# A transformer kernel without the products at its norms that nobody reads

## The chip, the cores and the metric

The kernel runs on one core of one Trainium2 chip. The metric is the device time of one launch in microseconds (us). All data are float32.
## What is computed

Two blocks in a row work on one sequence of 512 tokens with 1024 features. The first has two layers (a mixer of RG-LRU and mLSTM, then windowed attention), each with a convolved feed-forward part and a per-layer input; the second has two layers (MLA, then RWKV-7), each between two SwiGLU feed-forward parts, with gains and shifts that come from a conditioning vector. Ahead of every part stands an RMS norm:

```python
def rms_norm(x, g):
    xf = x.astype(jnp.float32)
    y = xf * lax.rsqrt(jnp.mean(xf * xf, axis=-1, keepdims=True) + EPS)
    return (y * g.astype(jnp.float32)).astype(x.dtype)
```

There are thirteen of them in the kernel, numbered 0 to 12. What follows each norm:

| norm | follows | first products on its result |
|---|---|---|
| 0 | mixer's inputs (`hy_in`) | 512 columns |
| 1, 4 | feed-forward, convolved (`up1`, `up4`) | 256 columns, with sums by VectorE |
| 2, 5 | per-layer input (`ple2`, `ple5`) | 512 columns |
| 3 | attention's inputs (`at_in`) | 512 columns |
| 6, 8, 9, 11 | SwiGLU (`up6`, ...) | 256 columns, with sums by VectorE |
| 7 | MLA's inputs (`mla_in`) | 512 columns |
| 10 | RWKV's inputs (`rw_in`) | 512 columns |
| 12 | the output | none |

## The kernel before

Activations lie transposed: features on the 128 partitions in 8 blocks (`X`, the residual, and `H`, the normed), tokens along the 512 columns. Weights stream as tiles of 16 blocks of 128 x 128 through a ring of three buffers (`weight_ring`), issued by SyncE. Each engine runs one program in written order and waits on semaphores; there is no scheduler. TensorE writes to eight PSUM banks.

A norm runs over all engines. ScalarE squares the eight blocks of the residual (`SQ`), VectorE adds the first six squares in `RB` (named `rstd` in rows, as the names go by buffer). TensorE's part is `norm_sum(n)`, from line 925:

- *the sums*: three times four products, over `RB` and the last two squares, each with `pick`, a matrix of 4 columns. In the rows they are 24 records of 4 columns (`constant_matrices,rstd` x8 and `constant_matrices,squares` x16), since a float32 product shows as two records;
- ScalarE takes the square root, VectorE the reciprocal (L2171) into four columns of `small_columns`;
- *the spread*: four products by the identity put it on all partitions (`constant_matrices,small_columns`, 8 records of 128 columns);
- VectorE then scales the eight blocks one after another (L2174), in norms 6 to 11 with a shift, which for block 0 VectorE adds (L2182) and for the others ScalarE. Each block's semaphore lets TensorE start on it.

Between these steps stand products of the identity with a constant matrix, written by the helper `fill(out, *widths)` (line 913): one product for each width (`T` is 512 columns, `HALF` 256), into `bank[0]` or the norm's own bank, before those banks are written anew. They bear no semaphore and wait for none. In norms 2 and 5 `ple_ahead` puts real products (the per-layer input) ahead of the sums and between sums and spread.

After norms 1, 4, 6, 8, 9 and 11 comes `up(n)`. It multiplies 2 x 2 blocks with seven products (`P1` to `P7`) in place of eight: P1 and P2 need normed blocks alone (8 products of 256 columns, 16 records), P6 and P5 need sums of blocks that VectorE makes once all eight blocks are normed (`token_sum`, L2203 to L2209).

Of the kernel before, what the change touches and what calls it, by code (L numbers as in the profile page):

```python
# [14 lines left out]
T = 512  # L15
# [280 lines left out]
CAT, NC = {}, 0  # L296
# [46 lines left out]
def build(nc, io):  # L343
    with ExitStack() as ctx:
        def sb(name, *shape):
            return ctx.enter_context(nc.sbuf_tensor(name, [P, *shape], F32))
# [3 lines left out]
        def S(name):  # L350
            if name not in names:
                names[name] = ctx.enter_context(nc.semaphore(name))
            return names[name]
# [13 lines left out]
        C = sb("constant_matrices", NC)  # L367
# [7 lines left out]
        bank = [ctx.enter_context(nc.psum_tensor(f"bank{b}", [P, T], F32)) for b in range(8)]  # L375
# [4 lines left out]
        def const(name, j=0, n=P):  # L380
            return C[:, CAT[name] + j * n:CAT[name] + (j + 1) * n]
# [9 lines left out]
        def sbank(s):  # L391
            return bank[4 + s % 4]
# [27 lines left out]
        norm_bank = bank[7]  # L420
# [25 lines left out]
        HALF = T // 2  # L446
# [214 lines left out]
        def _(sp):  # L661
# [49 lines left out]
            for n, (_, _) in enumerate(STREAM):  # L711
                if n == 2:
                    sp.dma_start(C[:, EARLY:], io["constants"][:, EARLY:]).then_inc(S("constants_landed"), 16)
                if n == rw_tile + 11:
                    store_low(0)
                    store_low(1)
                if n == rw_tile + 12:
                    store_low(2)
                    store_low(3)
                if n == rw_tile + 15:  # L720
                    store_inverses(0)
                    load_step(0)
                    load_step(1)
                if n == rw_tile + 17:
                    store_inverses(1)
                    for i in range(2, 16):
                        load_step(i)
                if n >= RING:
                    before = STREAM[n - RING][0]
                    if before is None:  # L730
                        sp.wait_ge(tile_used, plain_tiles(n - RING))
                    else:
                        part_is_full(sp, *before, "P4")
                for at, k, tile, place, *quarter in pieces(n):
                    lower = n == rw_tile + 6 and at == 8
                    rows, of = (slice(64, P), slice(0, 64)) if lower else (slice(0, P), slice(0, P))
                    for r in quarter:
                        rows, of = slice(32 * r, 32 * r + 32), slice(0, 32)
                    sp.dma_start(ring[rows, n % RING, at * P:(at + k) * P], tiles[tile][of, place * P:(place + k) * P])\
                        .then_inc(landed[n % RING], 16)  # L740
# [132 lines left out]
        def _(pe):  # L873
            at = {"m": 0, "s": 0, "w": 0, "free_inc": 0, "open": 0}

            def mm(out, lhsT, rhs, start, stop, inc=None):
                i = pe.matmul(out, lhsT, rhs, start=start, stop=stop)  # L877
                if inc is not None:
                    i.then_inc(inc, 1)
                elif at["free_inc"]:  # L880

                    i.then_inc(tile_used, at["free_inc"])
                    at["free_inc"] = 0
# [26 lines left out]
            def begin(name):  # L910
                assert (at["m"], at["s"], at["w"]) == AT[name], (name, at, AT[name])

            def fill(out, *widths):

                for n in widths:
                    pe.matmul(out[:, 0:n], const("ident"), C[:, CAT["sel"]:CAT["sel"] + n], start=True, stop=True)  # L916

            def ple_ahead(n, j):
                pe.wait_ge(S(f"p{n // 3}_landed"), 16)
                part_is_taken(pe, f"down{n - 1}", DB // 2 - 1, ("P7", "P4", "P3")[j])  # L920
                at["w"] = AT[f"ple{n}"][2] + 10 * j + 8
                for k in range(2):
                    mm(bank[4 + j][:, :], weight(), PT[:, k, :], k == 0, k == 1, S("ple_projected") if k else None)

            def norm_sum(n):

                begin(f"norm{n}")
                if at["s"] >= 4:
                    pe.wait_ge(small_done[3], at["s"] // 4)
                if n in (2, 5):  # L930
                    ple_ahead(n, 0)
                    ple_ahead(n, 1)
                if n in (3, 6):
                    fill(norm_bank, T, T)
                for k, x in ((5, RB[:, :]), (6, SQ[:, 0, :]), (7, SQ[:, 1, :])):
                    if k == 5:
                        pe.wait_ge(S("squares_added"), 5 * (n + 1))
                    else:
                        if k == 6 and n == 9:
                            fill(bank[0], T, T)  # L940
                        pe.wait_ge(S("square_ready"), DB * n + k + 1)
                    for t in range(NB):
                        mm(norm_bank[:, 0:NB], x[:, t * P:(t + 1) * P], const("pick", t, NB), k == 5 and t == 0,
                           k == 7 and t == NB - 1, S("norm_summed") if k == 7 and t == NB - 1 else None)
                if n in (2, 5):
                    ple_ahead(n, 2)
                    at["w"] = AT[f"ple{n}"][2]
                elif 0 < n < 12:
                    fill(bank[0], HALF)
                pe.wait_ge(S("rstd_ready"), n + 1)  # L950
                for t in range(NB):
                    mm(norm_bank[:, t * P:(t + 1) * P], RSTD[:, t:t + 1].to_broadcast([P, P]), const("ident"), True, True,
                       S("rstd_spread") if t == NB - 1 else None)
                if 0 < n < 12:
                    fill(bank[0], *((T,) if n < 6 else (T, T, T) if n == 10 else (T, HALF)))

            def project(rhs, kb, ready, cols=P, rows=P):

# [142 lines left out]
            def ple(n):  # L1101
                norm_sum(n)
                begin(f"ple{n}")
                w0 = at["w"]
                for j in range(DB):
                    at["w"] = w0 + 10 * j
                    project(lambda k: H[:, k, :], DB, normed(n) if j == 0 else settled)
                    if j >= AHEAD:
                        project(lambda k: PT[:, k, :], 2, settled)
                at["w"] = w0 + 10 * DB  # L1110
# [3 lines left out]
            for _ in range(5):  # L1114
                pe.matmul(bank[0][:, :], X[:, 0, 0:P], X[:, 0, :], start=True, stop=True)
            pe.wait_ge(S("first_constants_landed"), 16)
            norm_sum(0)
            begin("hy_in")
            h = lambda k: H[:, k, :]
# [92 lines left out]
            for j in range(DB):  # L1212
                project(y, DB, (lambda k: pe.wait_ge(S("y_rg"), k + 1) if k < 4 else pe.wait_ge(S("y_ml"), k - 3))
                        if j == 0 else settled)
            norm_sum(1)
            up(1)
            down(1)
# [40 lines left out]
            for w in range(16 + LAG + 1):  # L1258
                if w < 16:
                    n, g = w // 4, w % 4  # L1260
# [17 lines left out]
                if w >= LAG + 1:  # L1278
                    q = w - LAG - 1
                    n, g = q // 4, q % 4  # L1280
# [3 lines left out]
                    for b in range(0 if n else 1, 2):  # L1284
                        t = n - 1 + b
                        values = A[:, 12 + t // 2, t % 2 * 256 + 64 * g:t % 2 * 256 + 64 * g + 64]
                        for half in range(2):
                            turned = B[:, 12 + (2 * q + half) % 4, :].rearrange("p (e b t) -> p b e t", b=2, t=P)
                            out = sbank(ss[half])[64 * half:64 * half + 64, 0:256].rearrange("p (e t) -> p e t", t=P)
# [55 lines left out]
            for w in range(8 * NB + MLAG + 1):  # L1345
                if w < 8 * NB:
                    n = w % NB
# [15 lines left out]
                if w >= MLAG + 1:  # L1363
                    q = w - MLAG - 1
                    n = q % NB
# [1738 lines left out]
```

## Time and profile before

| | us |
|---|---|
| median of three runs | 4146.09 |
| lowest, highest | 4143.68, 4148.68 |
| the profiled execution | 4144.75 |
| its span, first to last instruction | 4142.9 |
| TensorE busy | 4024.5 (97%) |
| VectorE busy | 1971.4 (48%) |
| GpSimd busy | 1334.7 (32%) |
| ScalarE busy | 669.4 (16%) |
| mean granted clock of TensorE | 0.988 of 2.4 GHz |

Busy time of TensorE holds a modelled tail of each record, so that the records of a dense stretch overlap a little; the distance from start to start is what a record costs there. The windows of rows 2 begin with each norm's sums, at norms 0, 1, 2, 3, 7, 8 and 10; PE, PEld, DVE, ACT and POOL follow in this order. The profile's views used below are the page's parts, one source line's instructions, the timeline of an engine over a window, and sums over windows with the granted clock.

### The profile page before, as it was taken

To read this page: it belongs to the slowest core of one execution; us is meant where nothing else is said; L and a number is where in the kernel's file an instruction comes from. 1 tells how busy PE (TensorE), PEld (TensorE's weight loads), DVE (VectorE), ACT (ScalarE), POOL (GpSimd) and SP (SyncE) were. 2 spreads that over 40 slices of the span, in tenths; PEclk is the share of its full clock that TensorE was granted. 3 is DMA by queue.
4 is the path that set the end of the run, shared out by engine and by line. 5 is a ranking of instruction groups with operands and counts; after the bars stand their busy time and mean duration, and the time that the engine had idled before them with its cause. 6 is when DMAs were issued, how large, how long until landed. Compare 5 with 4: busy or idle time off the path is not lost. (4 is left out here: it accounts for less than half of the span.)

```text
span 4142.9 us, 45459 instructions
## 1 busy us (share of the span) xinstructions
PE 4024.5 (97%) x17988; PEld 3008.5 (73%) x17988; DVE 1971.4 (48%) x3520; ACT 669.4 (16%) x1404; POOL 1334.7 (32%) x1138
## 2 busy tenths in 40 slices
PE   9999999998899999999999999999999989989999
PEld 4448888644488885888844588888888437848888
DVE  5437766448377752433245344324432654434432
ACT  2321110114211101100024310001000321211000
POOL 0004444103244341344303434444443052023443
PEclk9999999999999999999999999999999999999999
DMA  3115454210244442222210122222222232112222
GB/s 130 41 66 188 159 181 163 81 66 24 92 172 173 141 174 72 81 83 89 84 66 21 41 88 85 87 87 82 82 87 87 71 111 63 32 47 92 82 87 76
DMA packets 133058, 386.80 MB, mean 93 GB/s; under 512 B 38800, under 2 KB 45072, under 8 KB 123120
## 3 DMA queue, kind: packets, MB, share of 16 engines
q1 hardware_dynamic: 118064, 305.23, 22.6%
q10 hardware_dynamic: 13968, 75.70, 4.9%
q8 instruction: 144, 2.36, 0.2%
q0 software_dynamic: 816, 2.97, 0.2%
q14 instruction: 66, 0.54, 0.0%
HBM read 375.26 MB, written 8.39 MB: 93 GB/s over the span
## 5 line engine op out<-in xcount | busy, mean ns | idle before, releaser
L877 PE MATMUL bank<-normed,weight_ring 128*128 128x256 f32 (+2 forms) x3376 | 1011.8, 453 | 17.8 <-ACT normed L1690 10.3
L877 PEld LDWEIGHTS bank<-normed,weight_ring 128*128 128x128 f32 (+1 forms) x3376 | 633.9, 189 | 359.5 <-issue 273.0
L877 PE MATMUL bank<-area_b,weight_ring 128*128 128x256 f32 (+3 forms) x2032 | 599.9, 442 | 5.2 <-issue 2.8
L877 PEld LDWEIGHTS bank<-area_b,weight_ring 128*128 128x128 f32 (+2 forms) x2032 | 378.9, 187 | 188.1 <-issue 147.9
L778 POOL TENSOR_TENSOR area_d<-weight_ring 128x512 f32<-128x512 f32 (+1 forms) x104 | 130.7, 1256 | 1073.4 <-PE bank L877 923.2
L877 PE MATMUL bank<-area_b 128*128 128x256 f32 (+2 forms) x1680 | 368.3, 377 | 13.1 <-DVE area_b L2796 11.7
L877 PE MATMUL bank<-area_a,weight_ring 128*128 128x256 f32 (+1 forms) x1360 | 372.2, 426 | 1.1 <-DVE area_a L2742 0.6
L877 PE MATMUL bank<-area_b,area_d 128*128 128x256 f32 x1536 | 351.7, 381 | 11.3 <-DVE area_b L2206 6.1
L877 PEld LDWEIGHTS bank<-area_b 128*128 128x128 f32 (+1 forms) x1680 | 304.5, 192 | 69.8 <-issue 14.6
L778 POOL TENSOR_TENSOR area_b<-weight_ring 128x512 f32<-128x512 f32 (+1 forms) x104 | 129.8, 1248 | 677.6 <-PE bank L877 652.9
L877 PEld LDWEIGHTS bank<-area_b,area_d 128*128 128x128 f32 x1536 | 292.3, 191 | 53.9 <-issue 14.3
L877 PEld LDWEIGHTS bank<-area_a,weight_ring 128*128 128x128 f32 x1360 | 256.1, 190 | 88.8 <-issue 57.4
L877 PE MATMUL bank<-normed,area_d 128*128 128x256 f32 (+2 forms) x1568 | 312.4, 352 | 0.0
L877 PE MATMUL bank<-normed,area_b 128*128 128x256 f32 x1184 | 279.7, 379 | 0.0
L877 PEld LDWEIGHTS bank<-normed,area_d 128*128 128x128 f32 (+2 forms) x1568 | 248.6, 177 | 36.4
L1690 ACT ACTIVATE area_d<-area_d 128x512 f32<-128x512 f32 (+2 forms) x153 | 88.4, 583 | 1078.5 <-DVE area_d L2647 917.2
L877 PEld LDWEIGHTS bank<-normed,area_b 128*128 128x128 f32 x1184 | 225.0, 190 | 30.6
L1690 ACT ACTIVATE temporary<-bank 128x256 f32<-128x256 f32 (+1 forms) x192 | 79.8, 416 | 986.4 <-PE bank L877 928.6
L2306 DVE SCALAR_TENSOR_TENSOR residual<-temporary,modulations,residual 128x256 f32<-128x256 f32 x64 | 45.4, 709 | 370.8 <-ACT temporary L1690 369.7
L2221 DVE SCALAR_TENSOR_TENSOR area_b<-area_b,small_columns 128x384 f32<-128x384 f32 x224 | 159.6, 712 | 7.9
L2632 DVE TENSOR_TENSOR area_d<-temporary,bank 128x256 f32<-128x256 f32 x88 | 37.0, 421 | 261.3 <-PE bank L877 261.3
L783 POOL TENSOR_TENSOR area_d<-weight_ring,area_d 128x512 f32<-128x512 f32 (+1 forms) x104 | 151.2, 1453 | 8.2
(324 smaller groups left out, 4966.9 us busy)
## 6 DMA issues: line engine op xcount, KB each, us to landing
weight_ring<-in_weights_dram SPq DMA_DIRECT2D x429, 512.0 KB, 4.6
area_b<-in_weights_dram ACTq DMA_DIRECT2D x48, 1024.0 KB, 5.0
weight_ring<-in_weights_dram SPq DMA_DIRECT2D x27, 1024.0 KB, 4.8
area_b<-in_weights_dram ACTq DMA_DIRECT2D x48, 512.0 KB, 6.2
weight_ring<-in_weights_dram SPq DMA_DIRECT2D x43, 384.0 KB, 4.4
weight_ring<-in_weights_dram SPq DMA_DIRECT2D x29, 256.0 KB, 4.1
weight_ring<-in_weights_dram SPq DMA_DIRECT2D x38, 128.0 KB, 4.0
low_scratch<-area_d SPq DMA_DIRECT2D x16, 256.0 KB, 2.1
```

The source lines that it names most:

```text
L778: po.tensor_tensor(s1, w21, w22, ALU.add).then_inc(S("pool_sum"), 1)
L783: po.tensor_tensor(s4, w12, s2, ALU.subtract).then_inc(weight_sums, 1)
L877: i = pe.matmul(out, lhsT, rhs, start=start, stop=stop)
L1690: return act.activation(out, in_, func, **kw)
L2221: i = ts(total, part, c, None, ALU.mult) if k == 0 else stt(total, part, c, total, ALU.mult, ALU.add)
L2306: return tt(x, x, part, ALU.add) if g is None else stt(x, part, g, x, ALU.mult, ALU.add)
L2632: tt(z_of(p)[:, half0], p1, part_bank("P2"), ALU.add).then_inc(part_taken, 1)
```

## The change

`fill` and its calls are removed from `norm_sum`: 33 products, 19 of 512 columns and 14 of 256 (norm 1: one of each; 2 and 5: one of 512; 3: three of 512 and one of 256; 4: one of each; 6 and 9: three of 512 and two of 256; 7, 8 and 11: one of 512 and two of 256; 10: three of 512 and one of 256; none in 0 and 12). No semaphore, wait, buffer or other instruction changes.

```diff
-            def fill(out, *widths):
-
-                for n in widths:
-                    pe.matmul(out[:, 0:n], const("ident"), C[:, CAT["sel"]:CAT["sel"] + n], start=True, stop=True)
-
...
                     ple_ahead(n, 1)
-                if n in (3, 6):
-                    fill(norm_bank, T, T)
                 for k, x in ((5, RB[:, :]), (6, SQ[:, 0, :]), (7, SQ[:, 1, :])):
                     if k == 5:
                         pe.wait_ge(S("squares_added"), 5 * (n + 1))
                     else:
-                        if k == 6 and n == 9:
-                            fill(bank[0], T, T)
                         pe.wait_ge(S("square_ready"), DB * n + k + 1)
...
                     at["w"] = AT[f"ple{n}"][2]
-                elif 0 < n < 12:
-                    fill(bank[0], HALF)
                 pe.wait_ge(S("rstd_ready"), n + 1)
...
-                if 0 < n < 12:
-                    fill(bank[0], *((T,) if n < 6 else (T, T, T) if n == 10 else (T, HALF)))
```

TensorE's order at norm 3, ahead of the attention's inputs (one row for a run of equal products; - is before alone):

```order
 L877 MATMUL bank<-per_layer_input,weight_ring 128x512 x2
-L916 MATMUL bank<-constant_matrices 128x512 x2
 L877 MATMUL bank<-constant_matrices,rstd 128x4 x4
 L877 MATMUL bank<-constant_matrices,squares 128x4 x8
-L916 MATMUL bank<-constant_matrices 128x256
 L877 MATMUL bank<-constant_matrices,small_columns 128x128 x4
-L916 MATMUL bank<-constant_matrices 128x512
 L877 MATMUL bank<-normed,weight_ring 128x512 x16
```

The sums now follow the per-layer input's products, the spread follows the sums, and the inputs' products follow the spread, with nothing between.

TensorE's order at norm 6, ahead of the up products (`area_b,area_d` is P6, the first that needs VectorE's sums); norms 8 and 11 read the same from the sums on:

```order
-L916 MATMUL bank<-constant_matrices 128x512 x2
 L877 MATMUL bank<-constant_matrices,rstd 128x4 x4
 L877 MATMUL bank<-constant_matrices,squares 128x4 x8
-L916 MATMUL bank<-constant_matrices 128x256
 L877 MATMUL bank<-constant_matrices,small_columns 128x128 x4
-L916 MATMUL bank<-constant_matrices 128x512
-L916 MATMUL bank<-constant_matrices 128x256
 L877 MATMUL bank<-normed,weight_ring 128x256 x8
 L877 MATMUL bank<-area_b,area_d 128x256 x8
```

Here the eight products of 256 columns on normed blocks come straight after the spread. The instructions of the other four engines stand as before.

## Rows read from the trace of the kernel before

**Rows 1.** The page, part 1 (us, share, instructions) and part 2 (TensorE's clock)
```profile
PE 4024.5 (97%) x17988; PEld 3008.5 (73%) x17988; DVE 1971.4 (48%) x3520; ACT 669.4 (16%) x1404; POOL 1334.7 (32%) x1138
...
PEclk9999999999999999999999999999999999999999
```
**Rows 2.** Sums at seven norms: window, us, five engines' busy us, PEclk, DMA, GB/s
```profile
10.68:23.68 13.00, 11.49 (x47) 7.10 (x47) 7.28 (x20) 5.40 (x9) 1.60 (x3) 0.87 0.96 382
307.88:320.88 13.00, 9.79 (x53) 6.77 (x51) 9.30 (x13) 1.28 (x3) 10.02 (x8) 1.00 0.36 124
781.63:794.63 13.00, 12.93 (x55) 7.58 (x54) 5.54 (x9) 1.55 (x2) 0.00 (x0) 1.00 0.00 1
854.74:867.74 13.00, 12.97 (x51) 7.81 (x52) 5.53 (x9) 0.89 (x2) 0.00 (x0) 0.87 0.36 121
...
2072.31:2085.31 13.00, 12.59 (x55) 7.39 (x54) 6.55 (x12) 6.20 (x10) 0.61 (x1) 1.00 0.33 120
2375.23:2388.23 13.00, 10.46 (x52) 7.95 (x51) 7.55 (x12) 6.23 (x11) 0.00 (x0) 0.87 0.23 81
...
3198.06:3211.06 13.00, 12.38 (x51) 8.17 (x50) 7.92 (x16) 3.69 (x6) 0.00 (x0) 0.87 0.24 78
```
**Rows 3.** Instructions of line 916, the fills (duration ns least/median/most)
```profile
L916 PE MATMUL bank<-constant_matrices x66: 379/592/1061, 310.5 to 3726.8; 128*128 128x512 f32 x38, 128*128 128x256 f32 x28
```
**Rows 4.** Timeline at norm 1: start us, us, engine, line, operation, [idle before]
```profile
311.19 1.16 PE L877 MATMUL bank<-constant_matrices,small_columns 128*128 128x128 f32 x8
312.18 1.02 PE L916 MATMUL bank<-constant_matrices 128*128 128x512 f32 x2
313.28 0.67 PE L877 MATMUL bank<-normed,weight_ring 128*128 128x256 f32 x2
...
320.95 3.69 PE L877 MATMUL bank<-area_b,area_d 128*128 128x256 f32 x16 [1.39 <-DVE area_b L2206]
...
310.95 0.18 DVE L2171 RECIPROCAL small_columns<-small_columns 128x4 f32<-128x4 f32 x1 [2.18 <-ACT small_columns L1690]
312.38 5.36 DVE L2174 SCALAR_TENSOR_TENSOR normed<-residual,vector_columns,bank 128x512 f32<-128x512 f32 x8 [1.25 <-PE bank L877]
```
**Rows 5.** Timeline of TensorE at norm 8
```profile
2376.04 1.93 PE L877 MATMUL bank<-constant_matrices,squares 128*128 128x4 f32 x16
2377.83 1.20 PE L916 MATMUL bank<-constant_matrices 128*128 128x256 f32 x2
2378.83 1.91 PE L877 MATMUL bank<-constant_matrices,small_columns 128*128 128x128 f32 x8
2380.53 1.81 PE L916 MATMUL bank<-constant_matrices 128*128 128x512 f32 x4
2382.20 0.67 PE L877 MATMUL bank<-normed,weight_ring 128*128 128x256 f32 x2
...
2386.81 2.43 PE L877 MATMUL bank<-normed,weight_ring 128*128 128x256 f32 x10 [0.62 <-ACT normed L1690]
2390.08 3.69 PE L877 MATMUL bank<-area_b,area_d 128*128 128x256 f32 x16 [0.84 <-DVE area_b L2206]
```
**Rows 6.** Sums over the low stretch at norm 8, columns as in rows 2
```profile
2377.83:2381.25 3.42, 3.42 (x13) 2.81 (x13) 0.65 (x2) 0.26 (x1) 0.00 (x0) 0.50 0.00 0
```
**Rows 7.** Timeline of VectorE at norm 8, the reciprocal
```profile
2378.31 0.18 DVE L2171 RECIPROCAL small_columns<-small_columns 128x4 f32<-128x4 f32 x1 [2.12 <-ACT small_columns L1690]
```
**Rows 8.** Timeline at norm 3: the first scaling, the first product
```profile
859.61 5.36 DVE L2174 SCALAR_TENSOR_TENSOR normed<-residual,vector_columns,bank 128x512 f32<-128x512 f32 x8 [1.51 <-PE bank L877]
861.07 9.37 PE L877 MATMUL bank<-normed,weight_ring 128*128 128x512 f32 x20
```
**Rows 9.** Sums over two stretches after norm 0, weight_ring's instructions alone (PE, PEld, POOL)
```profile
16.15:19.22 3.07, 3.07 (x4) 1.51 (x5) 0.00 (x0) 0.50 1.00 420
19.48:23.77 4.29, 4.29 (x11) 1.90 (x10) 0.00 (x0) 1.00 0.87 306
```
**Rows 10.** Sums over a stretch in RWKV's steps
```profile
3326.74:3333.56 6.82, 5.64 (x18) 2.88 (x20) 6.65 (x17) 3.12 (x11) 0.00 (x0) 0.50 0.15 56
```

## The prediction

> **What bounds the kernel now.** I read the page's engine line first: TensorE is busy 4024.5 of 4142.9 us and no other engine reaches half of the span, so what matters is TensorE's own work, its few idle places and its clock [rows 1]. The clock row shows 9 in every slice, that is 90% or more, and the span's mean is not quite full; a slice is over 100 us long and hides short falls. So the next view is the granted clock over 13 us from the start of each norm's sums [rows 2]. A mean of 0.87 over 13 us is 3.4 us at 1.2 GHz (0.13 x 13 x 2), 1.00 is none. Norms 1, 2, 7 and (not shown, same reading) 4 keep 2.4 GHz; norms 0, 3, 8, 10 and (not shown) 5, 6, 9, 11 have one stretch at 1.2 GHz. In all of them the sums that come first are 24 short records of 4 columns.
>
> Then the instructions to be removed: 66 records of line 916, two for each of 33 products, 38 of 512 columns and 28 of 256 [rows 3]; they bear no semaphore, so nobody waits for them. A pair of 512 columns takes 1.02 us at full clock [rows 4], and a pair of 256 1.20 us at the low one [rows 5]. If all of it were on the path it would be worth 19 x 0.86 + 14 x 0.43 = 22.4 us (0.43 us is the pitch of a 512-column record, 1.02 us less the 0.16 us of modelled tail, halved; 0.215 is half of it). So the whole question is what stands under these records, and what the clock does without them.
>
> **Where they stand.** In a norm the chain is: sums, square root on ScalarE, reciprocal on VectorE, the four products that spread the root, the eight scalings on VectorE, the first product on the result. The fills before the spread lie under the root and the reciprocal. In norm 1 the reciprocal ends at 310.95 + 0.18 = 311.13 and the spread starts at 311.19: no delay [rows 4]. The fills after it lie under the first scaling: that starts at 312.38, the first product at 313.28, 0.90 later [rows 4]. At full clock removing them saves nothing. At the low clock, which norm 8 has from 2377.83 to 2381.25 [rows 6], they stick out. In norm 8 the reciprocal ends at 2378.49 and the spread starts at 2378.83, 0.34 after it where norm 1 has 0.06: 0.28 us [rows 5, 7]. I take 0.28 for norms 8 and 11, 0.21 for 6 and 10, together 1.0. In norm 3 the first product starts 1.46 us after the scaling (859.61 to 861.07) where norm 1 has 0.90: 0.56 [rows 8]. **Direct gain: 1.5 us**; its bounds are 0 (those norms' clock high) and 3.
>
> **What the clock then does.** Norm 0 is the row without fills: sums, 0.66 idle, spread, 0.84 idle, then 512-column products, the first records of which run at the low clock: 3.07 us at 0.50 [rows 9]. Norm 8 has a low stretch too [rows 6], but its fills and the spread keep TensorE busy through it, and at 2382.20 the clock is back [rows 5]. The spread there takes 1.91 against 1.16 us in norm 1 [rows 4, 5]: 0.75 us, on the chain. Without fills I expect the fall in nearly every norm, since less work stands around the sums, and above all a later return, since between 2378.83 and 2386.81 only the spread and three pairs of records, each after a wait, would be left [rows 5]. What a later return costs depends on what follows the norm.
>
> - *Norms 3, 7, 10: dense 512-column products follow at once* (attention's, MLA's and RWKV's inputs). Low clock there is paid in full: a stretch like norm 0's, 3.07 us at half speed, costs 1.54 us. Three of them 4.6; and norm 7, now at full clock, also pays 0.75 for the spread: **5.4 us**. From below: half a stretch each, 2.3. From above: RWKV's steps have a stretch twice as long at 0.50, 6.8 us, after which TensorE was dense [rows 10]; all of it in dense work is 3.4 us each, 10.9 with norm 7's spread.
> - *Norms 6, 8, 9, 11: up products with VectorE's sums between.* TensorE takes ten 256-column records in 2.43 us and then waits 0.84 us for VectorE at 2390.08 [rows 5]. At the low clock these ten cost as much again, 2.2 us, of which 0.84 is covered: 1.36 if the clock is low throughout, 0 if it is back. I take half, 0.68 x 4 = **2.7 us**; bounds 0 and 5.4.
> - *Norms 1 and 4: the same with a wait of 1.39 us* [rows 4]. 2.2 - 1.39 = 0.8, half of it twice is **0.8 us**; and the spread, at full clock now, is low in about half of the cases: 0.75 x 2 / 2 = **0.8 us**. Bounds 0 and 3.1.
> - *Norms 2 and 5*: a product of the per-layer input stands between sums and spread and keeps TensorE busy; norm 2 stays at 1.00 with a single fill [rows 2]. Nothing, at most 1.5 each.
>
> Sum: -1.5 + 5.4 + 2.7 + 0.8 + 0.8 = **+8.2 us**. From the low ends: 2.3 - 3.0 = -0.7; from the high ends, with no direct gain: 10.9 + 5.4 + 3.1 + 3.0 = +22.4. The profiled execution took 4144.75 us (span 4142.9), 1.3 below the median of three; the falls do not sit at the same places in each execution, so I add the sum to both: 4153.0 for the profiled one, 4146.1 + 8.2 = **4154.3** for the median. Everything else is untouched: the order shows the fills gone on TensorE alone, no wait and no buffer changes, and the queues of the other engines are the same.
>
> **Rivals.** (a) *The fills carry nothing.* The clock falls during the sums, which stay, and the spread and the paced pairs bring it back as early as now. For it: in seven of the eleven norms with fills the fall comes in spite of them [rows 2]. Against: in norms 1, 2, 4 and 7 it doesn't come, and norm 0's runs on into the work. Then only the direct gain is left: 4146.1 - 1.5 = 4144.6. A rule of the Trainium skill ("TensorE: Matmul & The Clock Gate", section "Why this matters for your kernels") stands on this side: it asks for no long idle gap between bursts of products. Idle gaps in these norms without fills stay short, so by that rule the fills would be needless; but the trace shows the clock at 0.50 from 2377.83 on, with TensorE busy up to there without a gap, on the 4-column sums [rows 5, 6], so I give it little.
>
> (b) *The clock stays low into the dense part everywhere.* Price: one more low stretch of 3.4 us in dense work in each of nine norms (1, 3, 4, 6 to 11), half of 3.4 is 1.7, so 15 us on top of the direct part: 4146 + 15 = 4161, slower. The point from which it decides: the clock is still at 1.2 GHz when TensorE takes up the sums' products (2390.08 in norm 8). For it: the stretch of 6.8 us in rows 10. Against: after norm 0 the clock was back once 3.07 us of dense work had passed [rows 9].
>
> (c) *The fills are on the path*, by 8.4 us or more of their 22.4: faster. It would need most of the first products to be held up by them. Against: 0.06 us after the reciprocal in norm 1 [rows 4]; the delays found are 1.5 us.
>
> (d) *The change removes less than it says*: excluded by the order, all 33 are gone.
>
> **How the numbers follow.** A measurement of this kernel can tell about 0.2% from no change, 8.3 us, so the bound lies at 4154.4. Forecast 0.72: around +8.2, its own range halfway to either end, from +4 to +15, and about even on both sides of the bound: 0.37 within and 0.35 over. (a) 0.11, within. (b) 0.14, over. (c) 0.03. Slower 0.49, within 0.48, faster 0.03. Range: from between (a) and the forecast's low end, 4146, to (b) with a little over, 4163; left out are half of (a), (c) and the end of (b), under 0.2.
>
> **What would show it.** Windows of 13 us at norms 1, 4 and 7 read 0.87 or less, those of 3, 6, 8 to 11 below 0.87; norm 2 and 5 as now. The spread in norms 1, 4, 7 takes up to 1.9 us instead of 1.16 in some. The first 512-column pairs of norms 3, 7 and 10 have a pitch of 0.86 a record. In norm 8 the wait of 0.84 us before VectorE's sums is gone. VectorE's own durations don't change. It is wrong if norms read 1.00 without fills, or if TensorE's low stretches reach over 7 us in the dense part.

## The result: 0.48% slower, and the profile after

The changed kernel takes 4165.43 us (median of four, 4160.89 to 4166.6) against 4144.95 us for the kernel before on the same chip (4143.68 to 4148.68): a ratio of 1.0048, 95% interval 1.0036 to 1.0060. (Ratios here are estimated from all runs of both kernels, so they can differ a little from the quotient of the two medians.) That is 20 us more, where 8 were forecast, and above the stated range. The profiled execution has a span of 4159.1 us. The page, part 1 and part 2 (compare [rows 1]):

```profile
PE 4034.4 (97%) x17922; PEld 3020.1 (73%) x17922; DVE 1972.9 (47%) x3520; ACT 669.7 (16%) x1404; POOL 1335.0 (32%) x1138
...
PEclk9999999999999999999999999999999999999999
```

66 records are gone, 22 us of work, and TensorE is busy 10 us *longer*; the other engines' busy times stand. So what remains has become slower on TensorE. The mean granted clock of the whole span tells how much of it was at 1.2 GHz (before, then after):

```profile
core 0: 4142.9 us, clock 0.988
...
core 0: 4159.1 us, clock 0.976
```

Since the clock is either full or half, 0.988 means some 99 us at 1.2 GHz and 0.976 some 200 us. Another 100 us at half speed would cost 50 us if TensorE had been the limit in all of it; the spans differ by 16, so most of the added low time lay in waits or under other engines' work. The sums over 13 us from the start of each norm's sums, at norms 0, 1, 2, 3, 7, 8 and 10 (compare [rows 2]; the third number from the end is the granted clock):

```profile
10.80:23.80 13.00, 11.50 (x43) 6.97 (x44) 7.25 (x20) 5.40 (x9) 1.60 (x3) 0.74 0.92 375
308.12:321.12 13.00, 11.28 (x47) 8.13 (x46) 9.03 (x13) 1.28 (x3) 10.01 (x8) 0.66 0.33 100
780.23:793.23 13.00, 12.07 (x49) 7.36 (x48) 5.53 (x9) 1.55 (x2) 0.00 (x0) 0.87 0.01 1
855.12:868.12 13.00, 11.55 (x37) 8.79 (x38) 5.24 (x9) 0.84 (x2) 0.00 (x0) 0.50 0.20 62
...
2080.53:2093.53 13.00, 11.03 (x44) 7.22 (x43) 6.56 (x12) 6.19 (x10) 0.61 (x1) 0.74 0.35 122
2384.65:2397.65 13.00, 10.01 (x43) 7.22 (x42) 7.68 (x12) 5.86 (x10) 0.00 (x0) 0.61 0.24 81
...
3209.99:3222.99 13.00, 9.07 (x38) 6.18 (x37) 8.28 (x17) 3.82 (x7) 0.00 (x0) 0.63 0.24 80
```

Where before one stretch of 3.4 us or none was at 1.2 GHz, it is now half of these 13 us or more, except in norm 2 (0.87): norm 3 is at 0.50 throughout, norm 1 went from 1.00 to 0.66, norm 8 from 0.87 to 0.61. Two of the low stretches in full, at norms 8 and 6 (columns as above):

```profile
2387.47:2401.12 13.65, 10.74 (x26) 7.32 (x27) 10.37 (x14) 6.56 (x10) 0.00 (x0) 0.50 0.23 77
...
1667.26:1684.33 17.07, 13.83 (x45) 10.81 (x46) 9.04 (x18) 7.15 (x11) 0.00 (x0) 0.50 0.19 62
```

The timeline of TensorE at norm 8 (compare [rows 5]):

```profile
2384.65 0.95 PE L877 MATMUL bank<-constant_matrices,rstd 128*128 128x4 f32 x8
2385.46 1.93 PE L877 MATMUL bank<-constant_matrices,squares 128*128 128x4 f32 x16
2387.95 2.08 PE L877 MATMUL bank<-constant_matrices,small_columns 128*128 128x128 f32 x8 [0.57 <-DVE small_columns L2158]
2391.49 1.19 PE L877 MATMUL bank<-normed,weight_ring 128*128 128x256 f32 x2 [1.45 <-DVE normed L2169]
2393.46 7.27 PE L877 MATMUL bank<-normed,weight_ring 128*128 128x256 f32 x14 [0.79 <-ACT normed L1677]
2400.52 3.92 PE L877 MATMUL bank<-area_b,area_d 128*128 128x256 f32 x16
```

The pairs of 256 columns take 1.19 us instead of 0.67; from the second on they run into each other, as each takes nearly the 1.31 us that lie between one pair's block and the next; and the sums' products (`area_b,area_d`) start without the wait of 0.84 us that stood there, 1.29 us after VectorE's sum was ready (2398.00 + 1.23 = 2399.23). The row of that sum, from VectorE's timeline:

```profile
2398.00 1.23 DVE L2193 TENSOR_TENSOR area_b<-normed,area_b 128x1024 f32<-128x1024 f32 x1
```

The timeline of TensorE at norm 3, and the first scaling on VectorE:

```profile
855.12 1.84 PE L877 MATMUL bank<-constant_matrices,rstd 128*128 128x4 f32 x8 [3.07 <-DVE rstd L2178]
856.82 3.55 PE L877 MATMUL bank<-constant_matrices,squares 128*128 128x4 f32 x16
860.94 2.08 PE L877 MATMUL bank<-constant_matrices,small_columns 128*128 128x128 f32 x8 [0.56 <-DVE small_columns L2158]
863.90 2.90 PE L877 MATMUL bank<-normed,weight_ring 128*128 128x512 f32 x3 [0.89 <-issue]
...
863.05 5.36 DVE L2161 SCALAR_TENSOR_TENSOR normed<-residual,vector_columns,bank 128x512 f32<-128x512 f32 x8 [2.17 <-PE bank L877]
```

The same place before, with the two fills ahead of the sums:

```profile
851.60 1.88 PE L916 MATMUL bank<-constant_matrices 128*128 128x512 f32 x4
854.74 1.05 PE L877 MATMUL bank<-constant_matrices,rstd 128*128 128x4 f32 x8 [1.26 <-DVE rstd L2191]
855.65 1.93 PE L877 MATMUL bank<-constant_matrices,squares 128*128 128x4 f32 x16
```

In the changed kernel the clock is low from 854.89 on, that is already when the sums begin, after 3.07 us without work; before, the fills left 1.26 us of it. The 24 records of the sums take 5.25 us, with 4 columns each, where before they took 2.84 (854.74 to 857.58); in norm 8, where the clock falls only behind them, they take 2.74. Norm 6 has the same wait of 3.07 us, and its sums take 5.25 us for 2.92.

**Where the 20 us are.** From the timelines I took for each norm the time from the start of the last product ahead of it to the start of the 60th record behind its spread, and compared with before: norm 1 +1.0, 2 +1.7, 3 +4.3, 4 +0.9, 5 0.0, 6 +2.7, 7 +2.0, 8 +1.25, 9 +1.3, 10 +2.2, 11 -0.2 us, together 17.1. Norm 0, which has no fills in either kernel, differs by 1.8: its low stretch was 3.4 us in before's trace and is 6.8 here. That is not the change's doing: the seven other traces below of kernels that leave norm 0 as it is have 6.8 us (0.76 over the window of 10 to 24 us) in five and 10.2 us (0.63) in two, so before's trace happens to hold the shortest of nine. One of the two:

```profile
10.00:24.00 14.00, 10.79 (x39) 7.81 (x40) 7.02 (x13) 5.23 (x9) 1.60 (x3) 0.63 0.94 375
```

The rest of the difference of spans, 16.2 us, is the other stages, whose low stretches also stand at other places in each execution (-2.7).

### The profile page after: what moved, and what is told of

Same layout as the page of the kernel before. It is cut to its first block and busy times, and to the rows that moved or that the text cites. A ratio compares the mean times of both kernels' runs of the same rounds, so it can differ in the third digit from the quotient of the medians.

```text
span 4159.1 us, 45329 instructions
## 1 busy us (share of the span) xinstructions
PE 4034.4 (97%) x17922; PEld 3020.1 (73%) x17922; DVE 1972.9 (47%) x3520; ACT 669.7 (16%) x1404; POOL 1335.0 (32%) x1138
## 5 line engine op out<-in xcount | busy, mean ns | idle before, releaser
L877 PE MATMUL bank<-normed,weight_ring 128*128 128x256 f32 (+2 forms) x3376 | 1036.9, 462 | 18.6 <-DVE normed L2169 5.8
L877 PEld LDWEIGHTS bank<-normed,weight_ring 128*128 128x128 f32 (+1 forms) x3376 | 646.7, 193 | 368.4 <-issue 283.6
```

## The experiments

Theory C: what kept the clock at 2.4 GHz in the norms were the fills as products of many columns, and without them the clock falls in every norm and comes back late. Each time is compared with runs of before taken beside it (4145.5, 4145.4, 4144.9 us); single executions of before spread from 4139.1 to 4151.7 us, so a ratio is known to about 0.1%.

**The same fills with 4 columns.** About as long on TensorE at full clock, at the same places, with hardly any columns:

```diff
                 for n in widths:
-                    pe.matmul(out[:, 0:n], const("ident"), C[:, CAT["sel"]:CAT["sel"] + n], start=True, stop=True)
+                    for _ in range(n // P):
+                        pe.matmul(out[:, 0:4], const("ident"), C[:, CAT["sel"]:CAT["sel"] + 4], start=True, stop=True)
```

> The kernel before with every fill cut to 4 columns, at the same places and about as long on TensorE: four products of 4 columns (8 records of 0.11 us, 0.89 us) for one of 512 columns (0.86 us), two for one of 256. Theory C: the clock is held by products that stream many columns, so these fills carry nothing and the time is that of the changed kernel, about 20 us over before (at least +15). Rival I: what matters is that TensorE isn't idle between bursts of products; then these fills serve as well as the old ones and the time is that of before, within 3 us. Rival O: the loss comes from where instructions stand (queue, issue), not from the clock; then also within 3 us of before.

Measured: 4168.79 us, ratio 1.0054 (1.0040 to 1.0068), 23 us over before. Rivals I and O fall, the interval's lower end being 16 us over before: these fills are worth nothing. The timeline at norm 8 and the sums over its low stretch:

```profile
2395.80 0.93 PE L917 MATMUL bank<-constant_matrices 128*128 128x4 f32 x4
2396.59 2.06 PE L877 MATMUL bank<-constant_matrices,small_columns 128*128 128x128 f32 x8
2398.43 2.56 PE L917 MATMUL bank<-constant_matrices 128*128 128x4 f32 x12
2400.85 8.49 PE L877 MATMUL bank<-normed,weight_ring 128*128 128x256 f32 x16
...
2395.87:2409.52 13.65, 13.44 (x42) 10.33 (x42) 10.16 (x14) 6.60 (x10) 0.00 (x0) 0.50 0.23 78
```

By the profile's measure TensorE is busy for 13.44 of 13.65 us and yet at 1.2 GHz all the time. So being busy, as this measure has it, did not hold the clock here. At that clock these fills stick out: from the spread to the first product it is 4.26 us (2396.59 to 2400.85), in the changed kernel 3.54, which may be where this kernel's last 3 us over the changed one come from.

**Only the six ahead of sums** (norms 3, 6 and inside 9), given back to the changed kernel:

```diff
+                if n in (3, 6):
+                    fill(norm_bank, T, T)
...
+                        if k == 6 and n == 9:
+                            fill(bank[0], T, T)
```

> The changed kernel with the fills ahead of the sums given back in norms 3 and 6 and inside them in norm 9 (six products of 512 columns), nothing else. Theory C, from the two traces: the changed kernel ran the 24 records of the sums in norms 3 and 6 in 5.25 us against 2.84 and 2.92, because the clock had fallen in the idle 3 us ahead, and norm 9's last 16 in 2.55 against 1.94: 2.4 + 2.3 + 0.6 = 5.3 us on the chain. So 5 us less than the changed kernel, about +15 over before. Rival: the norms' low clock is all in the work after the spread; then these six carry nothing and the time is +20.

Measured: 4161.95 us, 1.0037 (1.0024 to 1.0049), +16.4 us. As theory C has it, but the interval reaches to +20, the rival's value, so this time alone doesn't decide between them. The trace shows what the rival denies, the sums of norm 3 back at 2.84 us; the kernel after the next settles it.

```profile
859.56 1.05 PE L877 MATMUL bank<-constant_matrices,rstd 128*128 128x4 f32 x8 [1.26 <-DVE rstd L2187]
860.47 1.93 PE L877 MATMUL bank<-constant_matrices,squares 128*128 128x4 f32 x16
862.97 2.08 PE L877 MATMUL bank<-constant_matrices,small_columns 128*128 128x128 f32 x8 [0.57 <-DVE small_columns L2167]
```

Norm 8 has no fills in this kernel either, and yet its low stretch is 10.2 us here for 13.65 in the changed kernel's trace, and P6 starts 14.72 us after the sums begin (2388.89 to 2403.61), which is 0.13 us less than before and 1.15 less than in the changed kernel.

```profile
2388.89 0.95 PE L877 MATMUL bank<-constant_matrices,rstd 128*128 128x4 f32 x8
...
2403.61 3.69 PE L877 MATMUL bank<-area_b,area_d 128*128 128x256 f32 x16
```

**Only those behind the spread**, given back to the changed kernel:

```diff
+                if 0 < n < 12:
+                    fill(bank[0], *((T,) if n < 6 else (T, T, T) if n == 10 else (T, HALF)))
```

> The changed kernel with the fills after the spread given back in norms 1 to 11, none ahead of it. Theory C: they bring the clock back before the first products, so the low clock in the work that follows (norms 1, 3, 4, 7, 8, 9, 10: 1 to 2 us each in the two traces, some 9 us) goes; the sums of norms 3, 6 and 9 stay slow (5.3 us) and so do spreads: about +8 over before. Rival: the clock returns only with what is dense after the norm, whatever stands behind the spread: +18 or more.

Measured: 4152.16 us, 1.0017 (1.0008 to 1.0026), +6.7 us; the rival's +18 is far outside. These 18 products carry two thirds of the effect. At norm 8 the spread is slow, but the first products are not, and VectorE is waited for again:

```profile
2382.19 2.07 PE L877 MATMUL bank<-constant_matrices,small_columns 128*128 128x128 f32 x8 [0.57 <-DVE small_columns L2165]
2384.05 1.96 PE L916 MATMUL bank<-constant_matrices 128*128 128x512 f32 x4
2385.84 0.59 PE L877 MATMUL bank<-normed,weight_ring 128*128 128x256 f32 x2
...
2393.59 3.69 PE L877 MATMUL bank<-area_b,area_d 128*128 128x256 f32 x16 [0.84 <-DVE area_b L2200]
```

**All but the six ahead of sums**: the kernel before less these.

```diff
-                if n in (3, 6):
-                    fill(norm_bank, T, T)
...
-                        if k == 6 and n == 9:
-                            fill(bank[0], T, T)
```

> The kernel before without the fills ahead of the sums in norms 3 and 6 and inside them in norm 9; all others stay. Theory C: only the sums of these three norms slow down, and the fills behind them bring the clock back: +5.3 us over before, +3 to +7. Rival: since the other fills stand close behind, the clock's fall there is cheap: within 1.5 us of before.

Measured: 4152.11 us, 1.0016 (1.0007 to 1.0025), +6.6 us, as theory C has it. The rival (within 1.5 us) falls: fills close behind don't make the early fall cheap, since most of the sums run at the low clock. At norm 3 they take 4.33 us, the last 16 records 3.45 for 1.93:

```profile
854.71 1.02 PE L877 MATMUL bank<-constant_matrices,rstd 128*128 128x4 f32 x8 [3.07 <-DVE rstd L2187]
855.59 3.45 PE L877 MATMUL bank<-constant_matrices,squares 128*128 128x4 f32 x16
```

This kernel and the one before it differ in the nine fills of 256 columns between sums and spread alone, and their times are equal: what those nine are worth is less than the 4 us or so that these intervals can tell.

**The changed kernel once more.**

> The changed kernel once more, for its place beside the kernel before on this chip and a second trace. Theory C: +18 to +21 us over before; the stretches at 1.2 GHz stand at other places than in the first trace, but again reach from the sums or the spread into the work behind each norm. Rival: the first trace's long stretches were chance, and this one has several norms at full clock.

Measured: 4163.94 us, 1.0043 (1.0030 to 1.0057), +18.6 us. The distances at the norms as above: 3 +4.4, 6 +2.6, 7 +1.9, 10 +2.2, 8 and 9 +1.2 each, 11 +1.2, 1 and 4 +1.0 and +0.8, 2 and 5 0.0: 16.5 together, and norm 0 +2.5. The long stretches aren't chance of one execution. Between these two traces only norms 2 and 11 differ, but what a single norm loses can differ from execution to execution elsewhere too, as norm 8 above shows (-0.13 against +1.25 and +1.2).

**Fills in norms 2, 3, 5, 7, 10 alone, and in norms 1, 4, 6, 8, 9, 11 alone.** The conditions of the kernel before are cut to these norms (shown for the first set; for the second the first condition reads `n in (6,)`, norm 9 keeps its two fills, and the other two read `n in (1, 4, 6, 8, 9, 11)`):

```diff
-                if n in (3, 6):
+                if n in (3,):
...
-                        if k == 6 and n == 9:
-                            fill(bank[0], T, T)
...
-                elif 0 < n < 12:
+                elif n in (3, 7, 10):
...
-                if 0 < n < 12:
+                if n in (2, 3, 5, 7, 10):
```

> The changed kernel with all fills given back in norms 2, 3, 5, 7 and 10, behind which dense products of 512 columns stand at once. Theory C, by the two traces, from the start of the sums (in 3 from the last product ahead) to a fixed record of the dense part: norm 3 lost 4.3, norm 7 2.0, norm 10 2.2, norm 2 1.7 us, together 10. Given back, what stays is the other norms' share: about +9 over before. Rival: work behind the up norms is what pays; then this kernel stays near +15.

> The changed kernel with all fills given back in norms 1, 4, 6, 8, 9 and 11, behind which the up products with VectorE's sums stand. Theory C, by the two traces: they lost 1.0, 0.9, 2.7, 1.25, 1.25 and -0.2 us, together 7, so about +12 over before; this and the kernel with the other norms' fills add up to the whole loss of about 20. Rival: losses of neighbouring norms aren't additive, because a shift by one changes where the clock falls in the next; then the two don't add up to 20 within their error.

Measured: 4157.03 us, 1.0024 (1.0016 to 1.0033), +11.7 us, with the fills in the first set; 4155.13 us, 1.0023 (1.0014 to 1.0032), +9.8 us, with those in the second. The first stays below its rival's +15, if not by much (the interval ends at +14). Both sets matter, and the two add up to 21 us, the whole loss within their joint error of about 5 us; the parts look additive as far as that can tell. Which set weighs more can't be told, the intervals being almost the same.

**More work of many columns** than before has:

```diff
+            def first_sum(n):
+                if at["s"] >= 4:
+                    pe.wait_ge(small_done[3], at["s"] // 4)
+                pe.wait_ge(S("squares_added"), 5 * (n + 1))
+                for t in range(NB):
+                    mm(norm_bank[:, 0:NB], RB[:, t * P:(t + 1) * P], const("pick", t, NB), t == 0, False)
...
-                    fill(norm_bank, T, T)
+                    fill(norm_bank, T, T, T)
...
+                    if k == 5 and n in EARLY_SUM:
+                        fill(pbank(at["m"] - 3), T)
+                        continue
...
-                elif 0 < n < 12:
+                elif n < 12:
...
-                if 0 < n < 12:
+                if n < 12:
```

`first_sum` is called from the last product of the stage ahead, and `EARLY_SUM` is norms 1, 4, 8 and 11; norm 0's fills multiply the residual's first block.

> The kernel before with more work of many columns around the sums: in norms 1, 4, 8 and 11 the four products over the first six squares go into the last product of the stage ahead, and a fill of 512 columns takes their place; norm 0 gets the two fills of norm 1; norms 3 and 6 get a third one ahead of their sums. Theory C: the clock no longer falls in norms 0, 1, 4, 8 and 11; a fall costs 0.75 us of spread and 0.3 us of fill there (1.5 us in norm 0), and comes in about two of three executions: 4 us under before, 1 to 6. Rival: the clock is already back where it matters, and the additions cost as much as they save: within 1 us of before.

Measured: 4144.37 us, 1.0000 (0.9991 to 1.0008). No gain shows, as the rival has it; the interval reaches to 3.7 us under before, so theory C's 4 us is out, a gain of 1 to 3 us is not. At norm 8 the clock no longer falls at the sums (the spread takes 1.16 us) but among the pairs behind it, and then the ten records before VectorE's sums are slow:

```profile
2376.62 1.16 PE L877 MATMUL bank<-constant_matrices,small_columns 128*128 128x128 f32 x8
2377.62 1.46 PE L919 MATMUL bank<-constant_matrices 128*128 128x512 f32 x4
2379.23 0.67 PE L877 MATMUL bank<-normed,weight_ring 128*128 128x256 f32 x2 [0.16 <-DVE normed L2202]
2381.21 0.70 PE L877 MATMUL bank<-normed,weight_ring 128*128 128x256 f32 x2 [1.31 <-ACT normed L1710]
2382.53 5.96 PE L877 MATMUL bank<-normed,weight_ring 128*128 128x256 f32 x12 [0.62 <-ACT normed L1710]
...
2382.11:2388.93 6.82, 6.31 (x14) 4.60 (x15) 6.00 (x7) 4.01 (x6) 0.00 (x0) 0.50 0.31 113
```

**And fills among those pairs, then in long waits elsewhere.** The second of these kernels holds the first:

```diff
+                            def ready(i):
+                                if what == "P1" and i:
+                                    fill(bank[1], *((HALF, HALF) if i == 1 and n >= 6 else (HALF,)))
...
+                if c == 0:
+                    fill(sbank(ss[0]), *({0: (T,) * 3, 3: (T,) * 8}.get(g, ())))
```

> The last kernel (more_fills) with one fill of 256 columns ahead of each of the second, third and fourth first product of the six up norms (two ahead of the second in norms 6, 8, 9 and 11), where TensorE waits 0.6 to 1.3 us for a normed block. Theory C: in more_fills the clock fell among these pairs (317.0 in norm 1) or stayed low through them (2382.1 to 2388.9 in norm 8); with more columns there it doesn't, and the first products and the spread run at full clock in most up norms: 2 to 4 us under more_fills, 3 to 5 under before. Rival: what these norms lose at 1.2 GHz is already hidden by VectorE's sums, so nothing changes: within 1 us of more_fills.

> pair_fills with fills in three long waits outside the norms, behind which dense work follows: 3 products of 512 columns in the wait of 3.7 us and 8 in that of 8.0 us of RWKV's low products, 2 in the 2.5 us ahead of the group norm's spread, 4 in the 4.5 us ahead of mLSTM's first sums. Theory C: the stretches at 1.2 GHz that follow these waits in before (203.5 to 210.4, 3326.7 to 3333.6, 3367.7 to 3374.5, 3647.6 to 3651.0; half of what of them is work: some 8 us) go: 5 to 8 us under pair_fills, about 10 under before. Rival: the fills hold back the work they stand ahead of, because the waits end earlier than the fills in some places: no gain, or slower than pair_fills.

Measured: 4145.67 us, 1.0001 (0.9992 to 1.0010), and 4147.72 us, 1.0001 (0.9992 to 1.0010). No gain shows either time: the 10 us that theory C had for wait_fills are excluded, of the 3 to 5 us for pair_fills all but the lowest end. In its trace pair_fills has full clock at norms 1, 4, 8 and 11. Still its norms are no shorter. What was added takes time of its own: the first eight records of the sums moved from the norm into the dense product ahead of it, and a fill of 0.86 us took their place. At norm 1, first before, then pair_fills:

```profile
307.88 0.95 PE L877 MATMUL bank<-constant_matrices,rstd 128*128 128x4 f32 x8
...
305.81 0.95 PE L877 MATMUL bank<-constant_matrices,rstd 128*128 128x4 f32 x8
306.62 3.68 PE L877 MATMUL bank<-area_b,weight_ring 128*128 128x512 f32 x8
310.14 1.02 PE L919 MATMUL bank<-constant_matrices 128*128 128x512 f32 x2
323.21 3.69 PE L877 MATMUL bank<-area_b,area_d 128*128 128x256 f32 x16 [1.43 <-DVE area_b L2229]
```

From 307.88 to P6 at 320.95 [rows 4] it was 13.07 us; from the fill at 310.14 to 323.21 it is 13.07 again, and the moved records' 0.81 us come on top, in a norm that had the full clock already. Taken over the same 120 records around the end of each spread (60 on either side, the moved ones within, fills not counted as records), norms 1 to 11 of pair_fills are together 1.0 us longer than before's: norms 1, 4 and 7 0.9 each (in 7, where nothing was added, the clock fell in this trace and not in before's), the others the same or up to 0.5 shorter. (This trace is also of the slowest of its eleven executions, 4151.66 us; the other stages, where it has the same instructions as before, lost the rest of the difference.) In wait_fills the fall at 3326.7 is gone, but another stands at 3336.7 to 3343.5, and the eight fills started late, because the bank they use came free only after 2.15 us:

```profile
3368.09 7.10 PE L919 MATMUL bank<-constant_matrices 128*128 128x512 f32 x16 [2.15 <-ACT area_d L1718]
3375.13 0.71 PE L877 MATMUL bank<-area_b 64*128 64x128 f32 x8
```

```profile
3373.55 1.11 DVE L2824 TENSOR_TENSOR area_b<-area_b,temporary 128x512 f32<-128x512 f32 x1
```

The last row is VectorE's result for which the low product waits, ready at 3374.66, so the fills held it back by 0.4 us. Why the rest of wait_fills' gain didn't come stays open. No version is shown to beat the kernel before.

## Why the prediction was wrong

The direction was right, and so was the mechanism that it named, a clock that comes back late; the size was under half of what was measured: +8.2 us against +20 and +18.6. By its own terms (distances of the two traces of the changed kernel, as above; of norms 3, 6 and 9 a part is the slower sums, 5.3 and 5.2 us together):

| term | predicted | measured at the norms | without the slower sums |
|---|---|---|---|
| norms 3, 7, 10 | +5.4 | +8.4, +8.5 | +6.0, +6.3 |
| norms 6, 8, 9, 11 | +2.7 | +5.1, +6.3 | +2.1, +3.3 |
| norms 1, 4 (both terms) | +1.6 | +1.9, +1.7 | +1.9, +1.7 |
| norms 2, 5 | 0 | +1.7, 0.0 | +1.7, 0.0 |
| fills ahead of and inside the sums | no term | in the rows above | +5.3, +5.2 |
| direct gain | -1.5 | about 0, in the rows above | |

- **The step that failed is that the fills ahead of the sums weren't priced at all.** "Where they stand" weighs the fills before and after the spread; that two products of 512 columns kept TensorE from 3 us of idle time ahead of the sums of norms 3 and 6, and that the sums run at half speed when the clock has fallen before them, is in no term. It is 2.4 us in norm 3 (5.25 for 2.84), 2.3 in norm 6 and 0.6 in norm 9, whose last 16 records took 2.55 for 1.94: 5.3 us, and the kernel without these six fills costs 6.6. With it rival (a)'s premise falls, that idle gaps in norms without fills stay short: these two are 3.07 us.
- **Second, the direct gain of 1.5 us came and was lost again at once.** At norm 3 the first product follows the scaling 0.85 us after its start (863.05 to 863.90), 0.61 sooner than the 1.46 before. At norm 8 the spread starts 0.05 us after the reciprocal, where it was 0.34. But the spread now runs at 1.2 GHz throughout: at norm 3 the scaling starts 2.11 us after the spread's start instead of 1.46, and from there to the first product it is 2.96 us for 2.92. The sum took the gain where the clock was low before and left out that there the spread would be low from end to end. With 5.3 us more and without this gain it would have given 15, inside the stated range.
- **The length of the low stretch was wrong, its price nearly right, and that is in part luck.** "A stretch like norm 0's, 3.07 us at half speed, costs 1.54 us": norm 0 of one execution was taken as the rule for a norm without fills, and it was the shortest of nine traces. In both traces of the changed kernel even norm 0 has 6.8 us, and norms 1, 3, 4 and 6 to 11 have 7 to 17 us; behind its first product norm 8 has 9.6 us of it (2391.49 to 2401.12), past the 7 in the dense part that the prediction itself gave as a sign of being wrong. But much of these stretches lies in waits: norms 7 and 10 lost 2.0 and 2.2 us in 6.8 and 10.2, and the terms of the late return come out within about 1 us each in the last column.
- **The half that was taken for norms 6, 8, 9 and 11** holds for their sum, not for each: norm 8 lost 1.25 us, nearly the upper bound of 1.36; norm 9 about 0.7 besides its sums, norm 6 0.4, and norm 11 -0.2 and +1.2. "The wait of 0.84 us before VectorE's sums is gone" came true at norm 8.
- **What is left of the 20 us**, 1.7 at norm 2 in one of the two traces and 2 to 3 outside the norms, is of the size by which single executions differ, and no run here pins it down.
- **The rivals.** (b), the clock low into the dense part everywhere, with 4161, was the nearest; it was given 0.14 because norm 0's clock came back early, the row that later traces show to be the exception. (a) fell with the result and the first experiment; so did what the Trainium skill's page "TensorE: Matmul & The Clock Gate", section "Why this matters for your kernels", suggests when read alone, that idle gaps are what has to be avoided: with fills of 4 columns there is no gap to speak of at norm 8, and the clock is at 0.50. At norms 3 and 6 of the changed kernel, though, the trace agrees with it: the clock had fallen after 3.07 us without work. (c) fell: less work, more time.
- **The direction of the chances**: slower had 0.49, the bound of 0.2% lying right at the forecast; with the terms at their measured size it is clear of it.

## What to carry to other kernels

Products that nobody reads can hold TensorE's clock through a stage of waits and narrow products, as they did here. Before they are taken out, go through them one by one, and price everything that comes behind each at half speed: here the sums behind the first of them were forgotten. Don't take the length of a low stretch from one trace; the same norm 0 showed 3.4, 6.8 and 10.2 us. In this kernel 4 columns for about as long a time did nothing, where 512 and 256 held the clock. And count what an added fill costs itself: more of them than before gave nothing here.

## What the runs showed of the hardware that I had not expected

- Records of 4 columns take twice as long at 1.2 GHz as well: eight of them 1.84 us against 0.95, though they stream next to nothing. Eight records of 128 columns take only 1.16 us at full clock [rows 4], so the time of the narrow ones is not in their columns, yet it goes with the clock.
- TensorE was at 1.2 GHz throughout a stretch in which, by the profile's measure, it was busy for 13.44 of 13.65 us (narrow_fills), with narrow records first and 256-column pairs then.
- The loss of the 33 fills was additive in parts within the error (11.7 and 9.8 us against 18.6 to 20 for both), although in every trace the falls stand at other places in the later stages.
